# One step of a hybrid two-layer decoder: norm scales applied after the product, the gated group norm done for four groups at once, early weight splits, and the expert output scaled on another engine

## The reference

```python
def rmsnorm(x, g):
    return x * rsqrt(mean(x * x, -1) + EPS) * g

# SSD, behind the recurrence: four groups of 512 channels, each with a norm of its own
yg = y * silu(z);  yg = yg.reshape(b, L, 4, 512)
yg = yg * rsqrt(mean(yg * yg, -1, keepdims=True) + EPS)
out = (yg.reshape(b, L, 2048) * gnorm_w) @ w_out

# dense FFN and every expert
gu = h @ w_gu;  out = (silu(gu[..., :f]) * gu[..., f:]) @ w_down

# SGU: u and v are 2048 channels each, ws is the lower triangle of w_s
uv = gelu(h @ w_in + b_in);  u, v = split(uv);  v = layernorm(v, ln_g, ln_b)
y = u * (ws @ v_chunk + b_s);  out = y @ w_out        # chunks of 128 tokens; v of the samples is an output too

# MoE
out = sum_e combine[:, e] * swiglu(h, w_gu[e], w_down[e])
```

## Time and profile before

| | us |
| --- | --- |
| median of 3 runs (1830.47 to 1832.38) | 1831.22 |
| the profiled execution's own time | 1833.29 |
| its span, first to last instruction | 1831.5 |
| TensorE busy in it | 1669.0 |
| VectorE (DVE) busy | 1360.4 |
| ScalarE (ACT) busy | 1071.4 |
| mean granted TensorE clock, of full speed | 0.960 |

### The profile page before, as it was taken

One profiled execution on the slowest core, in us unless ns is written; L12 is line 12 of the kernel. 1 busy time (PEld: TensorE's weight loads), 2 busy tenths in 40 slices (PEclk: granted clock), 3 DMA queues, 4 the chain that ended last, 5 costly groups with the idle time before them and its releaser, 6 DMA issues.

```text
span 1831.5 us, 24965 instructions
## 1 busy us (share of the span) xinstructions
PE 1669.0 (91%) x9200; PEld 1418.5 (77%) x9200; DVE 1360.4 (74%) x1364; ACT 1071.4 (58%) x1070; POOL 51.7 (3%) x90
## 2 busy tenths in 40 slices
PE   3889993889998989969999999999999999999994
PEld 2787772889997989857878878778788788787783
DVE  1866996555545656568888888788798888888886
ACT  1753344344433544337777777777777776777774
POOL 1000110000000000000000000000000000000000
PEclk9988997999999989979999999999999999999997
DMA  7432763496456444439999999999999999999994
GB/s 102 145 109 67 249 232 107 127 247 181 140 154 211 141 136 141 161 126 358 358 362 366 347 374 357 358 368 357 359 369 358 363 360 352 373 358 347 376 362 131
DMA packets 303945, 480.22 MB, mean 262 GB/s; under 512 B 10814, under 2 KB 151342, under 8 KB 303830
## 3 DMA queue, kind: packets, MB, share of 16 engines
q1 hardware_dynamic: 290736, 446.95, 71.0%
q0 software_dynamic: 7712, 27.62, 5.6%
q10 hardware_dynamic: 5432, 4.78, 0.9%
HBM read 461.19 MB, written 18.32 MB: 262 GB/s over the span
## 4 chain that ended last, share of the span: by engine, by line
PE 72%; DVE 11%; ACT 7%; issue 7%; DMA 2%; ACTq 0%; DVEq 0%; POOLq 0%; POOL 0%
PE bank L1177 9%; PE bank L1179 9%; PE bank L1178 9%; PE bank L809 7%; PE bank L810 7%; PE bank L811 7%; PE bank L1198 5%; PE bank L1200 4%; PE bank L1199 4%; ACT part L747 2%; DVE part L1709 2%; PE bank L1163 1%; DMA raw_w<-in_sgu_b_in_dram 1%; DVE part L331 1%; ACT part L324 1%
## 5 line engine op out<-in xcount | busy, mean ns | idle before, releaser
L1709 DVE TENSOR_TENSOR part<-raw_w,part 128x2048 fp32r<-128x2048 f32 x336 | 763.3, 2292 | 141.0 <-ACT part L747 119.7
L747 ACT ACTIVATE part<-raw_w 128x2048 fp32r<-128x2048 f32 x336 | 642.9, 1918 | 258.0 <-PE bank L1179 167.8
L1177 PE MATMUL bank<-part,xh 128*128 128x512 f32 x896 | 359.0, 401 | 10.7 <-DVE part L1709 9.2
L1179 PE MATMUL bank<-part,xl 128*128 128x512 f32 x896 | 354.8, 396 | 0.0
L1178 PE MATMUL bank<-part,xh 128*128 128x512 f32 x896 | 354.7, 396 | 0.0
L331 DVE TENSOR_TENSOR part<-raw_w,part 128x2048 fp32r<-128x2048 f32 (+1 forms) x84 | 181.7, 2166 | 138.2 <-ACT part L324 138.0
L809 PE MATMUL bank<-ah,part 128*128 128x264 f32 x800 | 238.4, 298 | 10.5 <-DVE al L1242 7.2
L810 PE MATMUL bank<-ah,part 128*128 128x264 f32 x800 | 232.2, 290 | 0.0
L811 PE MATMUL bank<-al,part 128*128 128x264 f32 x800 | 232.1, 290 | 0.0
L1177 PEld LDWEIGHTS bank<-part,xh 128*128 128x128 f32 x896 | 168.8, 188 | 53.5 <-DVE part L1709 12.2
L1179 PEld LDWEIGHTS bank<-part,xl 128*128 128x128 f32 x896 | 168.6, 188 | 40.6
(11 more groups left out here) (331 smaller groups left out, 1955.6 us busy)
## 6 DMA issues: line engine op xcount, KB each, us to landing
raw_w<-in_moe_w_gu_dram SPq DMA_DIRECT2D x226, 1024.0 KB, 7.2
raw_w<-in_moe_w_down_dram SPq DMA_DIRECT2D x112, 1024.0 KB, 7.2
raw_w<-in_ffn_w_gu_dram SPq DMA_DIRECT2D x44, 512.0 KB, 5.3
raw_w<-in_ssd_w_in_dram SPq DMA_DIRECT2D x20, 1024.0 KB, 5.6
raw_w<-in_sgu_w_in_dram SPq DMA_DIRECT2D x16, 1024.0 KB, 5.3
raw_w<-in_ffn_w_down_dram SPq DMA_DIRECT2D x16, 704.0 KB, 4.5
raw_w<-in_state_ssm_dram POOLq DMA_DIRECT2D x16, 512.0 KB, 5.4
out_dram<-raw_w POOLq DMA_DIRECT2D x16, 512.0 KB, 4.8
```

Of the source, the lines that this page charges most:

```text
L747: act.activation(part[:, n % PARTS, 0, :], raw_w[:, q, :], ACT.Copy).then_inc(S("part1"), 1)
L1177: mm(out, x[0], w[0][:, k, :], start=(half == 0 and k == 0), stop=False)
L1179: ins = mm(out, x[1], w[0][:, k, :], start=False, stop=(half == 1 and k == 3))
L1709: tt(part[:, n % PARTS, 1, :], raw_w[:, q, :], part[:, n % PARTS, 0, :].bitcast(F32), ALU.subtract).then_inc(S("part2"), 1)
```

## The change

1. **SSD.** Tiles 20 to 22 of `w_out` are loaded during the recurrence straight into the low half of a `part` buffer (`landing` is the same memory) and split there in place, by ACT at t = 9, 11, 13, by DVE at t = 10, 12 and once behind the loop. The transposes of the convolution state are done within the loop at six steps (`KEPT`), copied by ACT and sent out in six pieces. The group norm handles the four groups at once: gating and squares four blocks wide (128x1056), sums of all groups into one 4x264 tile by a selector matrix, one root and one reciprocal on four partitions, four TensorE products that spread each group's scale over 128 partitions, and the scaling from PSUM.
2. **Norms 1 and 2** (before FFN and SGU) are `LATE`: while the residual is formed, x·g is split without the token's scale. FFN results are multiplied by the scale afterwards (two more PSUM multiplications on DVE for a pair; silu reads SBUF; `hf` has three buffers). In the SGU the first four blocks (`HEAD`) use the unscaled split in four banks and are rescaled on DVE; meanwhile the scaled split is made for the others.
3. **Splitting ahead.** A semaphore at half of a down block lets the next tile be split then. Two roots' tables are loaded ahead of need.
4. **SGU middle.** The transposes of w_s, the row sums, the v transposes and the statistics are one to eight blocks later. The samples have a chain of their own, spread over blocks 17 to 24, with a root of their own; their v is transposed at blocks 25 to 28 and copied by ACT, and their gating is done in two pieces. `SPACE` starts a block later.
5. **MoE.** The loop's steps run from 1 to 42, so tile 2 of the next item is split at the end of a round, and the output's scaling goes from ACT to DVE, ahead of that split. The slot numbers of the next item are computed a tile later, and the two halves of its tokens' split are a tile apart or more.

The core of the diff:

```diff
+        EARLY = (20, 21, 22)
 (split_1)
+            if n in EARLY:
+                act.wait_ge(S("early_in"), 48)
+                act.activation(part[:, n % PARTS, 0, :], landing[:, n % PARTS, 1, :], ACT.Copy).then_inc(S("part1"), 1)
+                return
 (ACT, SSD loop)
+                    if t in KEPT:
+                        q = KEPT.index(t)
+                        act.wait_ge(S("misc"), misc + 1)
...
+                    if t in (9, 11, 13):
+                        split_1(act, 20 + (t - 9) // 2)
 (ACT, behind it)
-            for n in range(20, 23):
-                split_1(act, n)
             for g in range(G):
...
+                act.activation(sqg[:, g % 2], zT[:, 4 * g:4 * g + 4, :], ACT.Square).then_inc(S("sq_ready"), 1)
+            act.activation(spare, ones[:, 0:1], ACT.Sqrt).then_inc(S("groot_ready"), 1)
+            act.wait_ge(S("gms_ready"), 1)
+            act.activation(rs[0:G, 1, :], rs[0:G, 0, :], ACT.Sqrt).then_inc(S("groot_ready"), 1)
 (PE)
+                    ins = mm(psum[7][0:G, 0:T], gsel[:, g, :], sqg[:, g % 2, k, :], start=(g == 0 and k == 0),
+                             stop=(g == G - 1 and k == 3))
...
+                mm(psum[1 + g][:, 0:T], ident[0:G, g:g + 1].to_broadcast((G, P)), rs[0:G, 0, :], start=True, stop=True
+                   ).then_inc(S("gr_mm"), 1)
 (ACT, norm)
+                    if n in LATE:
+                        act.activation(a_out(n, m)[0], xT[:, m, :], ACT.Copy, scale=V[:, NORM[n] + m:NORM[n] + m + 1]).then_inc(
+                            S("ua1" if n == 2 else "a1"), 1)
 (DVE, FFN)
+                    tt(fs[:, n % 2, :], psum[2 * (n % 2)][:, 0:T], rs[:, 0, :], ALU.mult).then_inc(S("ffn_rs"), 1)
+                    tt(hf[:, n % 3, :], psum[2 * (n % 2) + 1][:, 0:T], rs[:, 0, :], ALU.mult).then_inc(S("ffn_rs"), 1)
 (PE, down)
+                        if per == 2 and c == 0:
+                            ins.then_inc(S("down_half"), 1)
 (PE, SGU; DVE)
+                x = (auh, aul) if n < HEAD else a12
...
+            def rescale(n):
...
+                tt(sq[:, n % 2, :], psum[bank_in(n)][:, 0:T], rs[:, 0, :], ALU.mult).then_inc(S("sgu_rs"), 1)
-                if n in (IT, IT + 1):
-                    k = n - IT
+                if n in (18, 21):
+                    k = n // 21
                     pe.wait_ge(S("vs_red"), k + 1)
-                if 22 <= n < 26:
+                if 25 <= n < 29:
 (ACT, MoE)
+            act.wait_ge(S("w_used"), 1)
+            split_1(act, ND + 2)
-                for s_ in range(ETILES):
+                for s_ in range(1, ETILES + 1):
...
-                    act.activation(yt[:, 512 * half:512 * half + 512], psum[4 + half][:, :], ACT.Copy,
-                                   scale=gatec[:, 0:1]).then_inc(S("e_y"), 1)
 (DVE, MoE)
+                    if s_ == ETILES:
+                        dve.wait_ge(S("w_used"), item * ETILES + (ETILES + 1))
+                        for half in range(2):
+                            ts(yt[:, 512 * half:512 * half + 512], psum[4 + half][:, :], gatec[:, 0:1], None,
+                               ALU.mult).then_inc(S("e_y"), 1)
```

More of the change, by code:

```diff
@@ L1260, in _ @@
             dve.wait_ge(S("vec_tr"), 1)
-            dve.nop().then_inc(S("start_over"), 1)
+            dve.nop().then_inc(S("ssd_stage"), 1)
+            step(dve.memset(gsel, 0.0))
+            own.did(dve.memset(small[:, 36:52:5], 1.0))
             dve.wait_ge(S("dtw_in"), 32)
@@ L1479, in _ @@
             residual(2, ahead_down)
[L1480 removed]
+            norm(2, G)
             U0 = D0 + 16
[L1483 to L1486 removed]
             def gated(n):
@@ L1531, in _ @@
                         own.did(dve.bn_aggr(vagg[:, c, :], vstat[:, c].rearrange("p t k -> p (t k)")))
+                    own.settle()
+                    step(ts(vvar[:, 0:2], vagg[:, :, 1], EPS, None, ALU.add))
+                    dve.nop().then_inc(S("vvar_ready"), 1)
+                    dve.wait_ge(S("vroot_ready"), 1)
+                    step(dve.reciprocal(vvar[:, 0:2], vvar[:, 0:2]))
+                    for c in range(2):
+                        ts(vtok[:, :, c, :], vtok[:, :, c, :], vagg[:, c, 0:1], vvar[:, c:c + 1], ALU.subtract, ALU.mult
+                           ).then_inc(S("vn_ready"), 1)
+                if n == IT + 4:
                     dve.wait_ge(S("vs_mm"), 1)
```

511 lines of the change are left out of this document (313 added, 198 removed).

## The result

The changed kernel takes 1757.1 us, median of 4 runs (1756.68 to 1757.73), against 1830.98 for the kernel before in the same comparison: a ratio of 0.9596, 95% interval 0.9579 to 0.9612. The forecast was 1779 within 1767 to 1793. The sign was right; the gain is 74 us where 52 were forecast, and the time lies outside the range.

What follows compares the result with a forecast made beforehand. TensorE was taken as the bound in FFN and MoE, serial DVE and ACT chains at the SSD's end and norms. Gains of 18.3 + 6.8 + 8.5 + 18.1 = 51.7 us gave 1781.6 profiled, 1779 as median; range 1767 to 1793.

Steps and rivals of the forecast that it cites:

- what bounds the kernel: Opening step: TensorE busy 1669.0 of 1831.5 us; no idle in the FFN, 123.07 of 124.83 us in a MoE item.
- mirror case: SGU and SSD: all unclear stalls gone, giving 1769 us; chance 12%.
- the three gaps: MoE: waits at the round's end, the down products and the slot numbers cost 1.58, 0.41 and 0.47 us.
- forecast cover of 1.2 us: MoE round's end: DVE scales, then finishes tile 2's split at 938.9, where it is needed at 940.1.
- The loads: First rival, MoE: loads bind instead of reaching the needed 366 GB/s; 18.1 us lost, 1797; chance 8%.
- SSD: End of the SSD stage: first output block picked up at 317.2 instead of 335.49, gaining 18.3 us; bounds 13 and 23.
- spreading products: SSD group norm: four products spreading the scales cost 1.8 us, an estimate between 0.7 and 3.3.
- Second norm and FFN: First FFN product starts near 380.4, 4.45 earlier, plus 2.3 of clock: 6.8 us; FFN pairs stay 5.8 apart.
- The FFN's ring: Third rival: split, multiplications, silu and copy take 6.7 us a pair, above 5.80; 20 lost, 1799; chance 4%.
- Third norm and SGU's start: First SGU product at about 585.7 instead of 592.85, gaining 7.1 us, net 7.0 after blocks 0 to 3.
- The SGU's middle: Stalls of 2.4, 4.0 and 3.4 us stay in blocks 21, 24 and 26 to 28; a gain of 1.5 us.
- GpSimd's scatter reads the same output about as early: MoE round's end: moving the output's scaling to DVE leaves the scatter's start about unchanged; no cost charged.

Runs made afterwards that it cites:

- e2: The changed kernel with `part` put back to byte 82048 and nothing else changed; 1777.6 us.
- e16: The changed kernel with `part` in place, but the normalised x, the experts' tokens and the arena 32 bytes further on; 1778.3 us.
- e11: The changed kernel without the semaphore at half of a down block, so the last splits ahead of the SGU wait for the whole block; 1762.6 us.
- e9: The changed kernel with the three remaining waits of the SGU's middle taken out by order alone, on DVE and ACT; 1749.26 us.

## Why the prediction was wrong, point by point

- **TensorE's own pace in the MoE.** The step that failed is the one under "what bounds the kernel": 123.07 of 124.83 us were read as work that nothing could shorten. The listing of the change has the lines that move `part`, and the prediction passed over them as bookkeeping. They are worth 2.76 us an item, or 20.5 us (e2) to 21.2 us (e16) of the kernel's time. None of the rivals held it: the mirror case only takes waits of the SGU and the SSD away, and all others were ways to gain less.
- **The MoE's order: right in kind, its cover by luck.** An inner item gains 2.51 at the old spacing (e2 against before), where the three gaps were forecast at 2.46. The forecast cover of 1.2 us took DVE as free when the last product ends. It is not: it is in the split of the tile before, as in the kernel before, until 933.80 + 2.29 = 936.09 where the prediction has the scaling done at 936.0. DVE's timelines of before and of e2:

```profile
933.80 2.29 DVE L1709 TENSOR_TENSOR part<-raw_w,part 128x2048 fp32r<-128x2048 f32 x1 [0.51 <-ACT part L747]
```

```profile
893.07 2.29 DVE L1893 TENSOR_TENSOR part<-raw_w,part 128x2048 fp32r<-128x2048 f32 x1 [0.51 <-ACT part L845]
895.28 1.41 DVE L1890 TENSOR_SCALAR moe<-bank,moe 128x512 f32<-128x512 f32 x2
896.60 2.28 DVE L1893 TENSOR_TENSOR part<-raw_w,part 128x2048 fp32r<-128x2048 f32 x1
```

The split of tile 2 ends at 898.88 and its first product starts at 899.32, so 0.4 us were left, and in the changed kernel, whose products are faster, 0.2 (896.86 and 897.05). The scaling that starts 1.4 us late costs nothing between items, but behind the last one it does: the MoE stage of e2 gains 16.6, not 18.1. At the new spacing the old order would have cost 3.27 an item.
- **The loads.** An item's window moved 376 GB/s against the 366 that the forecast needed. The Trainium skill's figure of some 358 (DMA: Bandwidth & Descriptors, section "Where 436 GB/s comes from") would have held an item's 44.9 MB at some 125 us, an estimate. The rows, 376 and 384 GB/s with TensorE never idle, speak against it here, as the forecast took it.
- **SSD: 20.5 instead of 18.3.** 1.1 us come ahead of the recurrence, where TensorE's wait ahead of the first decay sums is shorter (3.93 us instead of 6.27); not forecast. The recurrence grew by 4.6 (4.2 forecast). The chain behind it is 32.5 us long instead of 34, with two errors against each other. The sums of squares last until 298.1, 6.8 us behind the gating, where 3.6 were forecast for the last square and sums, since ACT's squares wait for TensorE at a clock of 0.79. The spreading products cost 0.9 instead of 1.8 (the bounds of that estimate, 0.7 and 3.3, don't follow from the 0.36 that it names: 4 x 0.36 is 1.4, doubled 2.9). The twelve hand-overs of 0.3, 3.6 in all, show by themselves only as DVE's wait of 0.5 ahead of the reciprocal; the others lie in the terms above. The two rows on DVE that answer to the earlier trace rows, one reciprocal of four rows and the pick-up:

```profile
299.03 1.79 DVE L1541 RECIPROCAL rs<-rs 4x264 f32<-4x264 f32 x1 [0.49 <-ACT rs L724]
...
314.95 0.43 DVE L1574 TENSOR_TENSOR xT<-xT,bank 128x264 f32<-128x264 f32 x1 [2.03 <-PE bank L902]
```

- **Second norm and FFN: right.** The first product starts at 359.52, with the last sums, at a clock of 1.00; pairs stay 5.80 apart (DVE's splits at 421.32 and 427.12). The FFN's ring never became the bound.
- **Third norm and SGU's start: too small by 2.2.** The first product stands 1.7 us behind the last down product, not 3.6: the step took DVE's split as done 2 us behind it, and it is done 0.5 us behind it (552.55 + 2.29 = 554.84). With 0.72 us of idle instead of the 4.7 and 2.7 of before the clock doesn't fall at all, a gain that the step had not counted. In e11, where it falls, the SGU's row is 6.7 us longer and the first product only 4.3 of them later, which leaves some 2.4 for the clock (an estimate). The other 1.4 us of the row in the table fit that, but no run separates them.
- **The SGU's middle: right in kind.** Forecast 9.8 us of idle in blocks 21, 24 and 26 to 28; measured 2.1 + 3.6 + 3.4 = 9.1, at the places named, each with the releaser named; e9 shows that they were the reason.
- **The end of the last item.** "GpSimd's scatter reads the same output about as early" was wrong by 3 us: the scatter starts 5.7 us behind the start of the last product instead of 2.6. Half of that is DVE's split ahead of the scaling (above), half GpSimd's step beside the next split: the prediction looked at the data and not at what each engine does at that moment.
- **The range** held the terms' errors (e2 would have been inside it) but had no room for a change in a stage's floor.

## What to carry to other kernels

When a change moves a buffer, ask who streams from it, even if the move is only there to make an alias possible; a shift of 32 bytes moved this kernel by 21 us (e16). A stage that is 99% busy has a floor that can move as well: compare the start-to-start time of its instructions, not only its idle. And before costing a chain on several engines, list what each engine still does beside the step that is moved: here DVE was still splitting when the scaling became possible, and GpSimd's one-element step met the next split. An idle of TensorE ahead of a stage can cost more than its length: behind 0.7 us the granted clock stayed at 1.00, behind 4.7 (e11) it fell and products started 0.22 apart instead of 0.12.

## What the runs showed of the hardware

- The spacing of 512-column fp32r products that follow each other with a weight load each was 0.227 to 0.234 us at a granted clock of 1.00, set by the distance between the two operands' places in SBUF; at a distance of 0 modulo 256 bytes it was 0.227 to 0.228, at 64 it was 0.229 and at the six others 0.232 to 0.234. With 264 columns no difference was seen (0.12 us in both kernels).
- A one-element GpSimd operation took 2.00 us beside a VectorE subtraction on SBUF and 0.19 without one; an indirect scatter's issue 2.68 and 1.58.
